# Weight slabs that meet the input before its norm is known, in a two-block transformer kernel on one core

## The reference

```python
def _rms_norm(x, g):
    y = xf * lax.rsqrt(jnp.mean(xf * xf, axis=-1, keepdims=True) + NORM_EPS)
    return (y * g.astype(jnp.float32)).astype(x.dtype)
...
        h = h + _rms_norm(merged @ w_out[l], norm_mix_post[l])
        f = _conv_ffn(_rms_norm(h, norm_ffn_pre[l]), ffn_w_up[l], ffn_conv_w[l], ffn_conv_b[l], ffn_w_down[l])
        h = h + _rms_norm(f, norm_ffn_post[l])
...
        h = modulate(rms_norm(x, ffn_norm[i, 0]), mod[:, 0, 0], mod[:, 0, 1])
        x = x + 0.5 * mod[:, 0, 2][:, None, :] * swiglu(
            h, ffn_w_gate[i, 0], ffn_w_up[i, 0], ffn_w_down[i, 0])
```

## Time and profile before

| | us |
|---|---|
| median of 3 runs | 2540.63 |
| lowest, highest | 2538.77, 2552.21 |
| the profiled execution's own time | 2553.17 |
| its span | 2551.4 |
| PE busy | 2347.3 |
| DVE busy | 1457.9 |
| ACT busy | 1061.8 |
| POOL busy | 800.2 |
| mean granted clock of TensorE, of 1 | 0.944 |

### The profile page before, as it was taken

How to read it: one execution, slowest core, us unless ns; L and a number is a source line. 1 busy time by engine, 2 the same in 40 slices (tenths; PEclk the granted TensorE clock), 3 DMA queues, 4 the chain that set the end, 5 groups by cost and what they waited for, 6 DMA issues and landing times.

```text
span 2551.4 us, 41098 instructions
## 1 busy us (share of the span) xinstructions
PE 2347.3 (92%) x16612; PEld 2149.0 (84%) x16612; DVE 1457.9 (57%) x2443; ACT 1061.8 (42%) x1930; POOL 800.2 (31%) x769
## 2 busy tenths in 40 slices
PE   6889889989998888989989989998899999988998
PEld 6677659879997677569889979987899999878998
DVE  4664556559847666466489654449544444435443
ACT  4444232245545443222455444432444444445443
POOL 2441002126624341012146434315243243221431
PEclk9998789989998998789989989999899999999999
DMA  6663237636674663247546745653356555533554
GB/s 211 169 174 105 96 103 263 231 99 215 217 237 125 184 176 105 89 154 266 195 144 223 243 137 183 183 155 132 118 188 182 158 184 183 170 121 119 187 180 126
DMA packets 121949, 429.27 MB, mean 168 GB/s; under 512 B 14960, under 2 KB 16928, under 8 KB 121633
## 3 DMA queue, kind: packets, MB, share of 16 engines
q1 hardware_dynamic: 94208, 333.80, 40.0%
q0 software_dynamic: 27408, 91.77, 12.5%
q10 hardware_dynamic: 144, 1.07, 0.1%
HBM read 425.48 MB, written 1.10 MB: 167 GB/s over the span
## 4 chain that ended last, share of the span: by engine, by line
PE 76%; DVE 12%; DMA 4%; POOL 4%; ACT 3%; issue 2%; DVEq 0%; ACTq 0%; POOLq 0%
PE bank L357 20%; PE bank L359 20%; PE bank L358 20%; PE bank L680 4%; DMA ada_ring<-in_ada 4%; PE bank L386 3%; DVE s_sb L1379 2%; POOL ring_lo L1987 2%; DVE std L1413 2%; PE bank L417 1%; DVE ring_lo L1391 1%; DVE s_sb L1418 1%; PE bank L347 1%; PE bank L508 1%; PE bank L550 1%
## 5 line engine op out<-in xcount | busy, mean ns | idle before, releaser
L357 PE MATMUL bank<-x_hi,ring_hi 128*128 128x256 f32 (+2 forms) x3552 | 1045.7, 294 | 70.7 <-DVE x_lo L1379 21.2
L358 PE MATMUL bank<-x_lo,ring_hi 128*128 128x256 f32 (+2 forms) x3552 | 1029.1, 290 | 0.0
L359 PE MATMUL bank<-x_hi,ring_lo 128*128 128x256 f32 (+2 forms) x3552 | 1026.1, 289 | 0.0
L1391 DVE TENSOR_TENSOR ring_lo<-ring,ring_hi 128x1024 fp32r<-128x1024 f32 (+1 forms) x437 | 593.7, 1359 | 609.7 <-ACT ring_hi L814 609.6
L357 PEld LDWEIGHTS bank<-x_hi,ring_hi 128*128 128x128 f32 x3552 | 688.6, 194 | 98.8 <-issue 21.2
L814 ACT ACTIVATE ring_hi<-ring 128x1024 fp32r<-128x1024 f32 (+1 forms) x551 | 570.2, 1035 | 376.6 <-PE bank L359 271.1
L359 PEld LDWEIGHTS bank<-x_hi,ring_lo 128*128 128x128 f32 x3552 | 690.3, 194 | 0.0
L358 PEld LDWEIGHTS bank<-x_lo,ring_hi 128*128 128x128 f32 x3552 | 688.6, 194 | 0.7
L1987 POOL TENSOR_TENSOR ring_lo<-ring,ring_hi 128x1024 fp32r<-128x1024 f32 (+1 forms) x155 | 373.0, 2407 | 816.4 <-ACT ring_hi L814 505.7
L359 PE MATMUL bank<-hid_hi,ring_lo 128*128 128x256 f32 (+1 forms) x1056 | 299.3, 283 | 0.0
L357 PE MATMUL bank<-hid_hi,ring_hi 128*128 128x256 f32 (+1 forms) x1056 | 298.1, 282 | 0.0
(11 more groups left out here) (275 smaller groups left out, 2290.4 us busy)
## 6 DMA issues: line engine op xcount, KB each, us to landing
ring<-in_w_gu SPq DMA_DIRECT2D x192, 512.0 KB, 3.5
ada_ring<-in_ada POOLq DMA_DIRECT2D x144, 512.0 KB, 5.2
ring<-in_w_in SPq DMA_DIRECT2D x136, 512.0 KB, 4.1
ring<-in_ffn_up SPq DMA_DIRECT2D x104, 512.0 KB, 3.5
ring<-in_w_down SPq DMA_DIRECT2D x64, 512.0 KB, 3.5
ring<-in_w_branch SPq DMA_DIRECT2D x32, 512.0 KB, 3.6
ring<-in_ffn_down SPq DMA_DIRECT2D x32, 512.0 KB, 4.1
ring<-in_w_down SPq DMA_DIRECT2D x32, 384.0 KB, 3.3
```

The lines of the kernel that those rows point to most:

```text
L357: pe.matmul(b[:, cs], ring_hi[:, i_hi, c0], x1, start=first and k == 0, stop=False)
L358: pe.matmul(b[:, cs], ring_hi[:, i_hi, c0], x2, start=False, stop=False)
L359: m = pe.matmul(b[:, cs], ring_lo[:, i, c0], x1, start=False, stop=last and k == nk - 1)
L1391: dve.tensor_tensor(ring_lo[:, i, 0:cols], ring[:, i, 0:cols], ring_hi[:, n % HIGH, 0:cols].bitcast(f32), ALU.subtract).then_inc(split(n)[ ...
```

## The change

It has three parts.

First, at top 0 and 1, FFN 0 and 1 and the four SwiGLUs, the first six slabs behind the norm (three steps j, `FZ = 3`) take `z`, the input times the gain but not divided by the root. ACT and DVE cut it into `z_hi` and `z_lo` (new `undivided`) as soon as a tile is final. DVE multiplies the bank by the reciprocal once the slab is done (new `scaled`), and only then may ACT or DVE read it. For the SwiGLUs two more columns (258 in place of 256) carry the shift, and DVE copies the column that results (`shifted`). The divided input, which the slabs from the seventh on need, is made meanwhile in three portions (`parts`), one at each of j = 0, 1, 2. At top 0 and 1, FFN 0 and 1 and s = 0 the squares' matmuls stand between those of the first slab (`first_slab`); at s = 2, 3 and 5 they follow it.

Second, at the norms behind the output projection and behind the FFN, and at s = 1 to 6, DVE adds the squares k = 1 to 6 to the first (`gather`) and PE makes two matmuls in place of 8 (`norm_gathered`). The table load for the root is put ahead of the last wait.

Third, the residuals of the first block are added by DVE (`added`), each followed by the low part of the tile before; POOL's two loops go. Gains of the norm behind a projection go into ACT's copy from the bank. The conditioning tiles in the FFNs move to later steps (from j = 13 on, and two at each of seven steps of the down-projection), their number stays. Small operations on the conditioning (`modulations`) are put into the last slabs of FFN 1.

```diff
+            def first_slab(name, b, cs, ready, norm_name, squares, ns):
...
+                for k in range(KD):
+                    pe.wait_ge(*at(*ready[k]))
+                    c0 = slice(k * P, (k + 1) * P)
+                    x1, x2 = z_hi[:, k, cs], z_lo[:, k, cs]
+                    pe.matmul(b[:, cs], ring_hi[:, i_hi, c0], x1, start=k == 0, stop=False)
+                    pe.matmul(b[:, cs], ring_hi[:, i_hi, c0], x2, start=False, stop=False)
+                    m = pe.matmul(b[:, cs], ring_lo[:, i, c0], x1, start=False, stop=k == KD - 1)
...
+                    pe.wait_ge(*at(act_, *squares, k))
+                    m = pe.matmul(ps[:, ns], ones, sq[:, k, ns], start=k == 0, stop=k == KD - 1)
...
             def swiglu(i):
                 s = (0, 2, 3, 5)[i]
-                norm(NB, ("in2", s), range(KD), [("sqx", s, k) for k in range(KD)], (act_, "std", "in2", s), TEXT)
...
+                        elif j + gv == 0:
+                            split_mm(name, claim(slab_bank(name), *by), z_hi, z_lo, 0, KD, SHIFTED, True, True, ready)
+                            norm_gathered(("in2", s), ("sqx", s, KD - 1), TEXT)
+                        elif j < FZ:
+                            project_z(name, SHIFTED, by)
...
+            def undivided(which, k, gain, hs, zs):
+                act.activation(z_hi[:, k, zs], h[:, k, hs], ACT.Identity, scale=gain, bias=0.0).then_inc(*sig(act_, "z_hi", *which, k))
...
                         halves(("gu", i, j, gv))
                         if gv == 0:
-                            act.wait_ge(*used(("gu", i, j, 0)))
+                            act.wait_ge(*scaled(("gu", i, j, 0)))
...
+                    for k in parts[j] if j < FZ else ():
+                        act.wait_ge(*at(dve_, "ux", s, k))
+                        act.activation(x_hi[:, k, 0:N2], u[:, k, 0:N2], ACT.Identity,
+                                       bias=mod[:, base + k:base + k + 1]).then_inc(*sig(act_, "xs", s, k))
...
+            def scaled(name, rs, cs=ALL):
+
+                b = bank[slab_bank(name)][:, cs]
+                dve.wait_ge(*used(name))
+                dve.tensor_tensor(b, b, rs, ALU.mult).then_inc(*sig(dve_, "scaled", *name))
...
+            def added(t, k, cs, rs, product, done, which, gain, zs):
+
+                dve.tensor_tensor(t[:, k, cs], t[:, k, cs], rs, ALU.mult).then_inc(*sig(dve_, *product, k))
+                dve.wait_ge(*at(dve_, *product, k))
+                dve.tensor_tensor(h[:, k, cs], h[:, k, cs], t[:, k, cs], ALU.add).then_inc(*sig(dve_, *done, k))
+                for x in ([k - 1] if k else []) + ([k] if k == KD - 1 else []):
+                    undivided(which, x, gain(x), slice(T - (zs.stop - zs.start), T), zs)
...
                 for j in range(NJ):
                     for gv in range(2):
-                        low_halves("up", l, j, gv)
+                        if j + gv:
+                            low_halves("up", l, j, gv)
+                        if j < FZ:
+                            scaled(("up", l, j, gv), rs, cs)
+                    for k in parts[j] if j < FZ else ():
+                        stt(u[:, k, cs], h[:, k, cs], par(l, "ffn_pre", k), rs, ALU.mult, ALU.mult, "uf", l, k)
+                    for k in parts[j] if j < FZ else ():
+                        dve.wait_ge(*at(act_, "x_hi", l, k))
+                        dve.tensor_tensor(x_lo[:, k, cs], u[:, k, cs], x_hi[:, k, cs].bitcast(f32),
+                                          ALU.subtract).then_inc(*sig(dve_, "x_lo", l, k))
+                    for gv in range(2):
                         w = par(l, "conv", 8 * j + 4 * gv, 4)
...
-                for k in range(KD):
-                    pool.wait_ge(*at(dve_, "uo2", l, k))
-                    pool.tensor_tensor(h[:, k, cs], h[:, k, cs], u[:, k, cs], ALU.add).then_inc(*sig(pool_, "h1", l, k))
```

308 lines of the change are left out of this document (208 added, 100 removed).

## The result

| | before | after |
|---|---|---|
| median of 4 runs each, us | 2543.48 | 2590.33 |
| lowest, highest | 2538.77, 2552.21 | 2580.35, 2595.90 |
| the profiled execution's own time | 2553.17 | 2580.35 |
| its span | 2551.4 | 2578.6 |
| mean granted clock | 0.944 | 0.938 |

The ratio is 1.0161, with a 95% interval of 1.0129 to 1.0193: slower by about 40 us, outside the range of the forecast. Between the two profiled executions the difference is 27.2 us.

A forecast was written before the change was run, and what follows sets the result against it. PE's matmuls, with idle holes at the norms, were taken as the bound. Terms 2.4 + 1.0 + 3.7 + 4.7 + 3 + 0.8 - 1 - 3.8 = +10.8 gave 2564.0 profiled, 2551.4 median; range 2508 to 2574.

The forecast's parts named there:

- Rival C: In FFN steps from the fourth, ring_lo ahead of the taps lengthens the loop: +15 to +30, 2556 to 2571; 30%.
- Two signs of being wrong: Stalls in the seventh slab under 4, or FFN steps 4 to 21 over 6.06 by more than 0.2.
- the latents' reciprocal: At the latents' norm in the mixers: within 2 us of its old distance from the last slab.
- Part 1: Until the first slab ends: 9 us won at both FFNs and s=0, 9.8 at s=2, 3, 5.
- Part 2: Slabs two to seven: PE stops about 8 us in the seventh, then slow clock; +0.8 each at s=2, 3, 5.
- the FFN terms: Norm to seventh slab: +3.7 in FFN 0, +4.7 in FFN 1; later loop steps +1 and +2.
- The norms of part 3: Gathered norms s=1, 4 and 6, nothing deferred: squares' matmuls shorten, -3.8 for three.
- Moved conditioning tiles: In FFNs and down-projections: 1.2 us each beside slabs of 3, costing nothing, or 3 if not; +3 in the sum.
- The +0.8 for top 1: Mixers of layer 1: DVE reaches the latents' reciprocal at about 799.4, not 798.59; bounds -7 and +2.
- The base: The profiled execution, 2553.17, was taken as 12.5 above the median of 2540.63.

The follow-up runs named there:

- ada_back: The changed kernel with the conditioning tiles on the schedule of before, all else as changed; ratio 1.0116.
- again: The changed kernel once more, unaltered, with a second profiled execution; 2583.12 us, ratio 1.0134.
- ffn_undone: The changed kernel with the deferral taken out of the two FFNs alone, conditioning tiles staying as changed; ratio 1.0053.
- undone_ada: The changed kernel with the deferral out of both FFNs and the conditioning tiles on the schedule of before; ratio 1.0006.
- extra_work: undone_ada with one more VectorE operation of about 1.2 us, needing no transfer, in each of the first seven down-projection steps; ratio 1.0012.
- gather_only: The kernel before with the gathered squares alone, nothing deferred, conditioning and residuals as before; ratio 0.9949.
- gather_first: The changed kernel with the add of the gathered squares ahead of the conditioning tiles in the down-projections; ratio 1.0119.

## Why the prediction was wrong

**Direction and size.** Forecast: within 0.5%, +10.8. Measured: +27.2 in the profile, +1.3 to 1.6% in the medians. Rival C had the sign, with 30%, but not the time (2556 to 2571), and its loops were the smaller part of the cause. Two signs of being wrong that the prediction named did not show: the stall was 6.28 and not under 4, and the loops ran over by 1.2 and 2.5 in 18 steps, under 0.2 a step. Of what it expected to see, one thing did not come: the latents' reciprocal, put within 2 us of its old distance from the last slab, was 6.3 further behind.

**Part 1 held in the main.** At s = 3 slab and squares ended 3.7 behind the last slab (forecast 3.8), at FFN 0 and 1 16.2 and 15.3 (15.7 and 15.3). At s = 2 and 5 they ended at 6.4, since the last residual, and so z_lo of tile 7, was late; at s = 0 at 16.9 (15.0), of which 2.30 is PE's wait for the last gathered square.

**Part 2 held in mechanism and nearly in size.** x_lo of tile 6 at 23.7 where 24.2 was forecast; a stall of 6.28 (forecast about 8, within 5 to 9) and half clock behind it; s = 2, 3 and 5 +1.3 together for +2.4, with part 1's loss of 2.6 at two of them inside; FFN 0 and 1 +2.9 and +4.2 for 3.7 and 4.7; their loops +1.2 and +2.5 for 1 and 2. That the FFN terms came out is in part luck: they were worked out without regard to where the tiles lie, and with the tiles on before's schedule (ada_back) the same stretches are 5.1, 4.8, 3.6 and 5.7. The Trainium skill (SBUF — State Buffer, "SBUF: two separate sides") calls the port that VectorE and GpSimd share an exclusive lock; that agrees with ring_lo at 2.21 and 2.76 beside POOL and 1.22 alone. What the prediction had not seen is that two chains run side by side, so that cutting one gives little: order or portions alone gave 1.5 to 2.5 a site, together no more than 3, POOL's share alone less than nothing, all three 7 to 9.

**The norms of part 3 held.** s = 1, 4 and 6 gave -1.5 (-3.0 in again; a mixer lies in it), -1.4 and -1.1 for -3.8 together. What failed is the last sentence of that part.

**The step that failed** is the one sentence "Moved conditioning tiles (as many as before, 1.2 each) lie beside slabs of 3: nothing, and 3 if they don't." It priced DVE's operation and not the transfer ahead of it, though two loads in each step instead of one were in the diff, and it did not ask how the engines come out of a deferred FFN. In place of 0 to 3 the runs showed 14.6 in the changed kernel: 2.4 in layer 0, 7.9 in layer 1, and 4.3 more in its last four slabs (of the 6.4 in that row; the last slab before the norm ended 24.6 behind, and the ring_hi at the start of those four slabs 20.3). That is most of the 16.4 between 10.8 and 27.2; the second profile of the changed kernel (again) has 13.7.

With the tiles on before's schedule 1.6 of the 14.6 are left (ada_back), with the deferral out of the FFNs 4.8 (ffn_undone), with both nothing (undone_ada). So most of the loss needs two things at once: two tiles in a step, whose transfers are late and have DVE's and POOL's ring_lo behind them, and a deferred FFN ahead. That the second acts through engines which come late to the down-projection fits POOL's ring_lo behind the FFN's last product (above), but was not tried by itself. DVE's operation was free where the FFNs were not deferred (extra_work). Putting the tiles back took 13.0 off the down-projections and put 8.5 on the FFNs. The larger decision by time was the deferral in the FFNs: 26 to 29 us of the stretches with them.

Behind the late tiles at top 1 PE waited 4.27 for the last gathered square; the latents' reciprocal was 12.3 late where the slab ahead of it was 6.0 late. The +0.8 for top 1 was wrong by 5.5, but by the end of the output projection behind the mixers this was gone: -0.4 over the whole stretch (4.0 in the second profile).

**Terms that were missing**: `modulations` ahead of the last gathered square at s = 0 (PE waits 3.54 for it in undone_ada, 0.77 in gather_only); and z_hi, z_lo and the gathered square beside each slab of the output projections. Ahead of s = 2 that was 1.0 and 0.4; ahead of s = 5 at most 1.8 and 5.3, mixer included.

**The base was wrong as well.** I took 12.5 off because the profiled execution stood that far over the median of three runs. The kernel before had medians of 2543.5, 2551.3, 2548.3, 2551.0, 2549.3 and 2552.5 in six groups, the first of which holds those three runs. The profiled 2553.17 was a usual execution, and the three runs happened to lie low. That moved the forecast of the median down by about 9.

**What stays open**: what deferral at top 0 and 1 is worth; how much cutting beside the output projection costs; and whether the tile is late for POOL's issue behind ring_lo or for the load on the transfers themselves (0.83 and 295 GB/s against 0.75 and 241). No run told these apart. For the tile shown in the trace after both had a part: DVE's multiply had freed its slot of the ring at 1483.2, POOL asked at 1489.46, 6.2 later, and the load then took 7.1, where the median of such loads is 5.3.

## What to carry to other kernels

When work is moved in an engine's list, price what it waits for, and what stands behind it: here 1.2 us operations were free where the FFN ahead was not deferred, while a second transfer ahead of them cost PE 5 us there, and 15 behind a deferred FFN. Deferring a division so that PE needn't idle pays only where the engines that catch up have the time: in two FFNs with VectorE busy 95 of 100 it cost 20 to 28 us, and in a SwiGLU it turned from nothing into 7 to 9 us a site once order, portions and POOL's share were all put right. One repair at a time showed each to be worth little, or less than nothing; a site with two chains needs both cut in one run. And when an experiment takes a loss out of one place, look whether it comes back in another: ada_back ended every wait for a tile in the down-projections, and the kernel was hardly faster.

## What the runs showed of the hardware

- DVE's sum of 128 x 272 with both inputs in SBUF took 2.58 beside POOL's ring_lo and 0.44 alone; POOL's ring_lo took 3.25 there and 2.4 alone. Both were longer in this meeting (gather_first, 767 us).
- The two profiled executions of the changed kernel differ in the mixers and nearly nowhere else. Of four kernels with the same code up to the second block, the stretch of the mixers of layer 1 was -1.8, -1.6, -2.3 and -9.6 against before, and the FFN and down-projection stretches agreed within 0.3. Here two single profiles gave a stretch without a mixer to less than 1 us and a total only to some 8.
- Six groups of the unaltered kernel before had medians between 2543.5 and 2552.5. Three runs are no base for a difference of 10 us.
